# A two-block transformer kernel on Trainium2: expert rows added in DRAM by the indirect store, rows normalised on GpSimd

## What is computed

```python
def hier_moe(h, ...):                        # per token: 1 of 4 groups, 2 of its 4 experts
    gates = ...                              # (512, 16), two non-zero values in a row
    a = einsum('td,edf->tef', t, w1)         # d = 1024, f = 256, e = 16
    c = einsum('td,edf->tef', t, w3)
    act = silu(a) * c * gates[:, :, None]
    y = einsum('tef,efd->td', act, w2)

y_moe = hier_moe(h, ...)
y_ple = sigmoid(h @ ple_wg + ple_bg) * (p @ ple_wp)
h = layer_norm_2(ALPHA * h + y_moe + y_ple, ln2_g, ln2_b)
```

## Time and profile before

| | |
|---|---|
| three runs | 2946.23 to 2948.44 us, median 2946.39 us |
| profiled execution | 2944.41 us, span 2942.6 us |
| TensorE busy | 95% of the span |
| VectorE, GpSimd, ScalarE busy | 62%, 52%, 37% |
| DMA | 338 MB, mean 115 GB/s |

### The profile page before, as it was taken

The page is one execution under the profiler, slowest core; times in us unless marked ns, Lnnn a source line. Parts: engine busy times, 40 slices in busy tenths (PEclk is TensorE's granted clock), DMA queues, the critical chain, the costliest instruction groups (busy, mean ns, idle before and its releaser), DMA issues. The chain is left out here.

```text
span 2942.6 us, 35447 instructions
## 1 busy us (share of the span) xinstructions
PE 2786.1 (95%) x12434; PEld 2181.6 (74%) x12434; DVE 1817.0 (62%) x2584; ACT 1098.4 (37%) x1899; POOL 1542.5 (52%) x929
## 2 busy tenths in 40 slices
PE   8999999999999999999999989999999799899996
PEld 6777778888877777778888867777676577677774
DVE  6887754443148877554431277667776585767775
ACT  3534333221025344232220134524555335434653
POOL 5544466666764543666666654665234344662241
PEclk9999999999999999999999899999999899999998
DMA  4222222333332212223333131135991321246942
GB/s 155 76 65 65 59 85 79 100 93 100 93 93 74 77 58 65 72 81 97 96 96 103 59 110 58 51 96 215 351 363 51 133 72 51 77 170 261 362 149 86
DMA packets 87032, 338.17 MB, mean 115 GB/s; under 512 B 19952, under 2 KB 22768, under 8 KB 77936
## 3 DMA queue, kind: packets, MB, share of 16 engines
q1 hardware_dynamic: 67744, 303.26, 31.1%
q0 software_dynamic: 17280, 26.26, 2.6%
q10 hardware_dynamic: 1872, 6.82, 0.6%
HBM read 371.91 MB, written 30.41 MB: 137 GB/s over the span
## 5 line engine op out<-in xcount | busy, mean ns | idle before, releaser
L179 POOL TENSOR_SCALAR wh<-ring 128x1024 fp32r<-128x1024 f32 x335 | 369.5, 1103 | 925.7 <-PE ps L240 723.4
L181 POOL TENSOR_TENSOR wl<-ring,wh 128x1024 fp32r<-128x1024 f32 x335 | 828.0, 2472 | 28.0
L238 PE MATMUL ps<-xh,wh 128*128 128x512 f32 x1720 | 691.5, 402 | 32.7 <-POOL xl L439 11.5
L239 PE MATMUL ps<-xl,wh 128*128 128x512 f32 x1720 | 675.4, 393 | 0.0
L240 PE MATMUL ps<-xh,wl 128*128 128x512 f32 x1720 | 674.7, 392 | 0.0
L238 PEld LDWEIGHTS ps<-xh,wh 128*128 128x128 f32 x1720 | 326.7, 190 | 112.1 <-issue 28.9
L239 PEld LDWEIGHTS ps<-xl,wh 128*128 128x128 f32 x1720 | 326.5, 190 | 70.0 <-issue 4.1
L240 PEld LDWEIGHTS ps<-xh,wl 128*128 128x128 f32 x1720 | 326.2, 190 | 69.8
L1432 DVE SCALAR_TENSOR_TENSOR taps<-ps,par,taps 128x511 f32<-128x511 f32 x192 | 143.8, 749 | 238.1 <-ACT taps L1162 223.2
L2850 DVE TENSOR_TENSOR ew_l<-ew,ew_h 128x1024 fp32r<-128x1024 f32 x184 | 213.1, 1217 | 0.0
L2418 ACT ACTIVATE ew_h<-ew 128x1024 fp32r<-128x1024 f32 x184 | 179.2, 1050 | 0.0
(11 more groups left out here) (518 smaller groups left out, 5196.4 us busy)
## 6 DMA issues: line engine op xcount, KB each, us to landing
ring<-in_w SPq DMA_DIRECT2D x343, 512.0 KB, 3.6
ew<-in_eu SPq DMA_DIRECT2D x32, 2048.0 KB, 9.8
ew<-in_ed SPq DMA_DIRECT2D x32, 1024.0 KB, 9.4
yg<-ypicks SPq DMA_DIRECT2D x16, 512.0 KB, 7.4
xrows<-xr ACTq DMA_DIRECT2D x8, 512.0 KB, 2.6
z<-in_x SPq DMA_DIRECT2D x4, 512.0 KB, 4.4
gw<-in_gw SPq DMA_DIRECT2D x2, 1024.0 KB, 6.7
out<-z SPq DMA_DIRECT2D x8, 256.0 KB, 2.9
```

The costliest lines, as they stand in the source:

```text
L179: nc.gpsimd.tensor_scalar(hi, raw, 1.0, 0.0, ALU.mult, ALU.add).then_inc(sem["w_hi"], 1)
L181: nc.gpsimd.tensor_tensor(lo, raw, hi, ALU.subtract).then_inc(sem["w_split"], 1)
L238: nc.tensor.matmul(out, wh, xh, start=first, stop=False, **kw)
L239: nc.tensor.matmul(out, wh, xl, start=False, stop=False, **kw)
```

## The change

The indirect store no longer copies a row but adds it to the row that stands in DRAM (`compute_op=ALU.add`). The target is a new array `yrows` of 512 rows, one per token, addressed by the same `idx` as the gather; the table `dst` goes. Since two tiles can hold the same token, each store waits for the landing of the one before. `yrows` is filled beforehand with the tokens themselves, by four further DMAs on ScalarE's queue, so `z` needs only ALPHA - 1 times the token. Reading back takes one DMA a quarter. VectorE's two additions become one with the row sum, and the normalisation goes to GpSimd, which waits for the reciprocal (`tk_rstd`).

```diff
@@ SyncE, after the last tile
                     for c in range(4):
-                        for q in range(2):
-                            row = (4 * q + c) * P
-                            sp.dma_start(yg[:, 2 * c + q, :], ypicks[row:row + P, :]).then_inc(sem[f"yg_in{c}"], 16)
+                        sp.dma_start(yg[:, 2 * c, :], yrows[c * P:c * P + P, :]).then_inc(sem[f"yg_in{c}"], 16)
@@ GpSimd
-                    g.wait_ge(sem["xrow_out"], at("xrow_out", 16 * 4))
+                    g.wait_ge(sem["xrow_out"], at("xrow_out", 32 * 4))
...
-                        nc.gpsimd.indirect_dma_start(ypicks[:, :], bass.IndirectOffsetOnAxis(ap=dst[:, j:j + 1], axis=0),
+                        if j:
+                            g.wait_ge(sem[f"y_out{(j - 1) % 2}"], at(f"y_out{(j - 1) % 2}", 16 * ((j - 1) // 2 + 1)))
+                        nc.gpsimd.indirect_dma_start(yrows[:, :], bass.IndirectOffsetOnAxis(ap=idx[:, j:j + 1], axis=0),
                                                      (y_b if j % 2 else y_a)[:, :], None,
-                                                     bounds_check=PICKS - 1, oob_is_err=False).then_inc(sem[f"y_out{j % 2}"], 16)
+                                                     bounds_check=S - 1, oob_is_err=False, compute_op=ALU.add
+                                                     ).then_inc(sem[f"y_out{j % 2}"], 16)
...
                     if layer + 1 < DEPTH:
                         g.wait_ge(sem["dn_mm"], at("dn_mm", TILES))
                         split_apart(g, nc, sem, sh, u0 + U2 + SPLIT, apart)
+                    for c in range(4):
+                        g.wait_ge(sem["tk_rstd"], at("tk_rstd", c + 1))
+                        nc.gpsimd.tensor_scalar(yg[:, 2 * c, :], yg[:, 2 * c, :], tk[:, 1, c:c + 1], tk[:, 4, c:c + 1], ALU.add, ALU.mult
+                                                ).then_inc(sem["tk_norm"], 1)
@@ ScalarE
                             act.dma_start(xrows[t * P:t * P + P, :], xr[:, t, :]).then_inc(sem["xrow_out"], 16)
+                            act.dma_start(yrows[t * P:t * P + P, :], xr[:, t, :]).then_inc(sem["xrow_out"], 16)
@@ VectorE
-                    do(V.tensor_scalar(dst[:, :], place, float(NOWHERE), None, ALU.add))
...
-                            do(V.scalar_tensor_tensor(z[:, j, :], z[:, j, :], ALPHA, spec[:, j, :], ALU.mult, ALU.add))
+                            do(V.scalar_tensor_tensor(z[:, j, :], z[:, j, :], ALPHA - 1.0, spec[:, j, :], ALU.mult, ALU.add))
...
-                        dve.wait_ge(sem[f"yg_in{c}"], at(f"yg_in{c}", 32))
-                        V.tensor_tensor(yg[:, 2 * c, :], yg[:, 2 * c, :], ps[:, 2 * c:2 * c + 2, :].rearrange("p a b -> p (a b)"), ALU.add
-                                        ).then_inc(sem["zt_taken"], 1)
-
-                    def row_sum(c):
+                        dve.wait_ge(sem[f"yg_in{c}"], at(f"yg_in{c}", 16))
+                        V.scalar_tensor_tensor(yg[:, 2 * c, :], yg[:, 2 * c, :], 1.0, ps[:, 2 * c:2 * c + 2, :].rearrange("p a b -> p (a b)"),
+                                               ALU.mult, ALU.add, accum_out=tk[:, 0, c:c + 1]).then_inc(sem["zt_taken"], 1)
                         dve.wait_ge(sem["zt_taken"], at("zt_taken", c + 1))
-                        do(V.scalar_tensor_tensor(yg[:, 2 * c, :], yg[:, 2 * c + 1, :], 1.0, yg[:, 2 * c, :], ALU.mult, ALU.add,
-                                                  accum_out=tk[:, 0, c:c + 1]))
                         V.tensor_scalar(tk[:, 1, c:c + 1], tk[:, 0, c:c + 1], -1.0 / D, None, ALU.mult).then_inc(sem["tk_mean"], 1)

                     def row_norm(c):
                         dve.wait_ge(sem["tk_std"], at("tk_std", c + 1))
-                        do(V.reciprocal(tk[:, 4, c:c + 1], tk[:, 3, c:c + 1]))
-                        V.tensor_scalar(yg[:, 2 * c, :], yg[:, 2 * c, :], tk[:, 1, c:c + 1], tk[:, 4, c:c + 1], ALU.add, ALU.mult
-                                        ).then_inc(sem["tk_norm"], 1)
+                        V.reciprocal(tk[:, 4, c:c + 1], tk[:, 3, c:c + 1]).then_inc(sem["tk_rstd"], 1)
```

More of the change, by code:

```diff
@@ L1464 @@
 ROWS_E = EXPERTS * P
-PICKS = 2 * S
 NOWHERE = 8192
@@ L1509 @@
         "picks": 1, "rank_mm": 1, "slot_mm": 1, "slots": 1, "spare_ready": 1, "idx_ready": 1, "half_ready2": 1, "xrow_mm": 8,
-        "xrow_evac": 8, "xrow_out": 16 * 4, "xgt_mm": TILES, "xgt_lo": 2 * TILES, "xgt_hi": 2 * TILES, "up_mm": UP_PARTS * TILES,
+        "xrow_evac": 8, "xrow_out": 32 * 4, "xgt_mm": TILES, "xgt_lo": 2 * TILES, "xgt_hi": 2 * TILES, "up_mm": UP_PARTS * TILES,
         "e_hi": UP_PARTS * TILES, "e_lo": UP_PARTS * TILES, "silu": TILES,
         "hact": TILES, "hactt_mm": TILES, "hactt": TILES, "dn_half": TILES, "dn_mm": TILES, "y_lo": TILES, "y_hi": TILES,
-        "zt_mm": 4, "zt_taken": 4, "tk_mean": 4, "tk_sq": 4, "tk_std": 4, "tk_norm": 4, "xt_mm": 8, "pg_sig": C8, "pp_done": C8, "pt_hi": 4, "pt_lo": 4,
+        "zt_mm": 4, "zt_taken": 4, "tk_mean": 4, "tk_sq": 4, "tk_std": 4, "tk_rstd": 4, "tk_norm": 4, "xt_mm": 8, "pg_sig": C8, "pp_done": C8, "pt_hi": 4, "pt_lo": 4,
         **{f"xg_in{n}": 16 * turns_of(TILES, n, 2) for n in range(2)}, **{f"y_out{n}": 16 * turns_of(TILES, n, 2) for n in range(2)},
@@ L1516, with second_block @@
         **{f"es_{w}{n}": 16 * turns_of(TILES - EXPERTS, n, 2) for w in ("up", "dn") for n in range(2)},
-        **{f"yg_in{c}": 32 for c in range(4)}}
-def second_block(nc, mem, sh, sems_before, d_cst, d_tab, d_w, first_unit, d_par, d_p, d_pw, d_rt, d_eu, d_ed, xrows, ypicks, out):
+        **{f"yg_in{c}": 16 for c in range(4)}}
+def second_block(nc, mem, sh, sems_before, d_cst, d_tab, d_w, first_unit, d_par, d_p, d_pw, d_rt, d_eu, d_ed, xrows, yrows, out):
     with ExitStack() as ctx:
@@ L1588, in second_block @@
         slot_gate = at_("slot_gate", 195.84375, [P, TILES])
-        dst = at_("dst", 195.9375, [P, TILES], I32)
         spare = at_("spare", 196.0625, [P, TILES - EXPERTS], I32)
@@ L1619, in second_block @@
                  "dn_half", "dn_mm", "y_lo", "y_hi", "y_out0", "y_out1", "yg_in0", "yg_in1", "yg_in2", "yg_in3", "zt_mm", "zt_taken",
-                 "tk_mean", "tk_sq", "tk_std", "tk_norm", "xt_mm", "pg_sig", "pp_done", "pt_hi", "pt_lo", "pq_mm", "pq_evac", "stored", "in_rstd", "in_rows", "consts"])
+                 "tk_mean", "tk_sq", "tk_std", "tk_rstd", "tk_norm", "xt_mm", "pg_sig", "pp_done", "pt_hi", "pt_lo", "pq_mm", "pq_evac", "stored", "in_rstd", "in_rows", "consts"])
         sem, sem_range = sems(nc, ctx, names)
@@ L2923, in row_norm @@
                         dve.wait_ge(sem["tk_std"], at("tk_std", c + 1))
-                        do(V.reciprocal(tk[:, 4, c:c + 1], tk[:, 3, c:c + 1]))
-                        V.tensor_scalar(yg[:, 2 * c, :], yg[:, 2 * c, :], tk[:, 1, c:c + 1], tk[:, 4, c:c + 1], ALU.add, ALU.mult
-                                        ).then_inc(sem["tk_norm"], 1)
+                        V.reciprocal(tk[:, 4, c:c + 1], tk[:, 3, c:c + 1]).then_inc(sem["tk_rstd"], 1)
                     for c in range(4):
                         pick_rows(c)
-                        row_sum(c)
                         if c:
@@ L2951, in build @@
         xrows = nc.dram_tensor("xrows", (S, D), F32, kind="Internal").ap()
-        ypicks = nc.dram_tensor("ypicks", (PICKS, D), F32, kind="Internal").ap()
-        second_block(nc, mem, sh, sem_range, d["cst2"], d["tab"], d["w"], DEPTH * U1, d["par2"], d["p"], d["pw"], d["rt"], d["eu"], d["ed"], xrows, ypicks, out)
+        yrows = nc.dram_tensor("yrows", (S, D), F32, kind="Internal").ap()
+        second_block(nc, mem, sh, sem_range, d["cst2"], d["tab"], d["w"], DEPTH * U1, d["par2"], d["p"], d["pw"], d["rt"], d["eu"], d["ed"], xrows, yrows, out)
 def _blocks(w):
```

## The result

The changed kernel takes 2951.59 us (median of 18 runs, 2946.07 to 2956.39) against 2946.48 us (18 runs) for the kernel before on the same chip: ratio 1.0018, 95% interval 1.0011 to 1.0024. Forecast were 2933.5 us and 12.8 us less than before; measured are 5 us more. That is 18 us from the forecast. It lies inside the given range of 2929 to 2955 only because the range had been drawn wide enough to hold rival (b). The whole interval lies above 1, but the difference is smaller than the 0.2% that the prediction took as the least that can be told.

The account below looks back on a forecast made before the run. TensorE, with work for 95% of the span, sets the pace. Layer ends give -7.0 and -6.8 us, adding stores cost 1.0, together -12.8 us: median 2933.5 us, range 2929 to 2955.

Parts of the forecast that it names:

- rival (b): Loaded tiles: store chain costs about the end's gain, 2.3 to 9.4 us a layer, 2937 to 2951 us; chance 0.10.
- The end of the layer: Reading back and normalising after the last store: TensorE released earlier, by 7.0 us in layer 0 and 6.8 in layer 1.
- The front of the layer: Before the first gather: four added copies, earlier idx, moved clearing of pool and fewer reads change nothing, 0 us.
- The price of the adding stores: Expert tiles: adding instead of copying rows costs TensorE 0.5 us a layer, with 0 and 2 as ends.
- The DMA time itself: Adding stores' extra work on the DMA engines: from nothing up to 12 us more a layer, some 11 on loaded tiles.
- The 5% and 9% of idle DMA time: Loaded tiles: idle DMA time of 7.5 us in layer 0, 12.6 in layer 1, leaves a backlog of at most 3.5.
- The store then also meets a shorter queue: Loaded tiles: a landing above 10.05 us delays the next store, which then finds less queued; no separate size given.
- rival (a): Loaded tiles: 13 chained stores run slower than the tiles; landing of 11.5 us costs 13.6 a layer, 2960 us; chance 0.21.

## Why the prediction was wrong, step by step

**The end of the layer** held. TensorE's idle time is 9.97 and 9.94 us (forecast about 10.4), the passes on VectorE stand 1.53 us apart (2303.53 to 2308.12; forecast 1.6), GpSimd's pass takes 1.19 us (taken: 1.05; bounds 0.81 and 2.06; all eight took 1.19 to 1.20, also beside VectorE's new pass). From read to release it is 7.75 us less in layer 0 (forecast 7.0). Of that, 0.90 went back: the transposes took 6.05 us until ScalarE could start, not the 5.15 that I kept, because the granted clock stood at 0.50 until 2315 where before it had risen by 2313. In layer 1 the whole end is 8.00 us shorter (forecast 6.8). The two layers gave 14.85 us against 13.8, and the run in the new order without wait and addition shows it in the medians.

**The front of the layer** held: the first gather stands 1.65 us earlier than before in the trace, which tells nothing (in the kernel with the new order it stands at 2046.20, 9 us later, with the same copies), and nobody waits for the added copies.

**The price of the adding stores** is the step that failed: "I enter 0.5 us a layer, with 0 and 2 as ends." It was 10.07 and 8.38 us: landings passed what a link of the chain allows, where the prediction had the chain cost nothing that reaches TensorE. One part of its argument held, the others went wrong.
- *The DMA time itself was bounded well*: 12 us more a layer as upper bound, 13.3 measured (half of 26.6, good to 1.5). The Trainium skill, Collectives: The Full Stack, "The bandwidth ceiling: the fold count and why AG ≠ RS ≠ AR", has the add of a collective read two sources through one ring, which halves the rate; the trace agrees with the factor, with 6.1 us per MB in place of 2.9. That the cause is the second source is not shown: the profile counts as many bytes for the adding stores as for the copying ones.
- *The 5% and 9% of idle DMA time were counted as room.* In layer 0 little of it was: without the wait the share over the same 140 us rose only from 0.96 to 0.97, and landings grew by 8.3 us from the first store to the thirteenth (8.0 to 16.3), where in the kernel before they grew by 2.3 (7.3 to 9.6). That is 6 us, 0.5 us a tile; the added work is 12.2 / 16 = 0.76 us a tile by the bound, 0.83 by the measured price. So more than half of it went into the backlog, which was at least 6 us and not 3.5. In layer 1 the share rose from 0.91 to 0.96, and the landings had a median of 12.5 us.
- *"The store then also meets a shorter queue"* fell. Under the wait, landings did not shrink with lateness: from the second store to the seventh they are 11.8, 12.8, 11.2, 9.6, 10.2 and 10.6 us, all but the first of them of late stores. A reading of this, not tested by itself: SP refills the queue with weights as TensorE leaves them, so a late store finds the queue as long as ever. It fits that the weights, too, landed no sooner (median 10.1 us in that stretch, 9.4 before).
- *Two terms were missing.* The latency of the adding store itself had no row, as rival (a) says, and the forecast put it at nothing; it is 0.5 to 3 us on the late tiles. And to each landing come 0.85 us until the next store starts, which the formula of rival (a) left out: it set L against 10.05, where landing + 0.85 has to stay below it.

With the true link in it, rival (a)'s own formula gives no more than the order of size. The first 12 loaded stores stand 11.37 us apart in layer 0 and 11.36 in layer 1 (2697.97 to 2822.92), hence 13 x 1.32 - (16.8 - 11.37) = 11.7 us a layer, 23 together. All 13, with the short last interval, give 11.01 and 10.98, hence 6.7 and 6.3 us, 13 together. 18.45 were lost. So the mechanism that came true is that of rivals (a) and (b), with a time at (b)'s upper end: 2951 was its last value. That the end of the layer gave 1 us more than forecast had no part in the miss. I had given both together 0.31, when the share of 0.95 and the median of 9.3, 0.1 us above what a link allows, spoke for them.

## What to carry to other kernels

A wait for a DMA's landing in every turn of a loop makes a chain of landing plus some 0.85 us; hold that sum, and not the landing, against the turn, and use the landing under the load that the change itself creates. DMA engines with an idle share of 5 to 9% had little room here: more than half of the added work went into the landing of what was behind it. The wait alone can be free or not by a small margin: with copying stores it cost nothing in one kernel and 5 us of a layer in another. An order of the work in which the conflicting items lie apart can replace such a wait: here it turned 1.0018 into 0.9982, which, alone or with the repeated transposes (0.9977), is the fastest version with the full computation that was run.

## What was unexpected of the hardware

- On loaded tiles, the instruction that issues an indirect store keeps GpSimd for 1.59 to 1.60 us (medians; 1.74 without the wait) when the store adds, against 1.15 us when it copies.
- The clock fell a second time. After the shorter wait it stood at 0.50 until 2315, was 1.00 for the end of the transposes, and fell again while TensorE waited for `xl`; the next layer began at the 1.2 GHz level (granted clock 0.50), its first matmul taking 0.77 us and not 0.47. In the changed kernel:

```profile
2313.00:2315.00 2.00, 2.00 (x12) 2.00 (x11) 0.00 (x0) 0.00 (x0) 0.55 (x1) 0.51 0.00 0
2315.00:2317.00 2.00, 0.80 (x8) 0.56 (x6) 0.06 (x1) 1.54 (x3) 0.00 (x0) 1.00 0.00 0
2317.00:2319.00 2.00, 0.00 (x0) 0.00 (x0) 1.33 (x2) 2.00 (x4) 0.00 (x0) 0.84 0.00 0
2319.00:2325.00 6.00, 5.88 (x14) 4.66 (x15) 2.81 (x5) 6.00 (x10) 0.00 (x0) 0.50 0.00 0
```

In the kernel before the last of these windows shows 28 matmuls at 1.00. It costs little in the end: the whole stretch from the next layer's first matmul to layer 1's first gather is 1.22 us longer.
